# ScalarE and VectorE take over Pool's work in and around the layer norms of a decoder layer

## The chip, the cores and the metric

The kernel runs on one core of a Trainium2 chip. The metric is the device time of one execution, in microseconds; lower is better. Engines: TensorE (PE, and PEld for its weight loads), VectorE (DVE), ScalarE (ACT), GpSimd (POOL) and SyncE (SP), which issues nearly all DMAs.

## What is computed

One decoder layer on 560 tokens: 16 learned meta tokens and 512 prompt tokens, and 8 sequences of 4 new tokens with a cached window of 128. The model width is 1024, the hidden width of a feed-forward 2816, all in float32. Cut to what matters:

```python
def trunk_layer(x, ...):
    x = layer_norm(DN_ALPHA * x + 0.5 * swiglu(x, wg[0], wu[0], wd[0]), g[0], b[0])
    y, ks, vs, cs = token_mixer(x, ...)          # attention and short convolution, then w_out
    x = layer_norm(DN_ALPHA * x + y, g[1], b[1])
    x = layer_norm(DN_ALPHA * x + 0.5 * swiglu(x, wg[1], wu[1], wd[1]), g[2], b[2])

def layer_norm(x, g, b):
    mu = mean(x); var = mean((x - mu) ** 2)
    return (x - mu) * rsqrt(var + eps) * g + b
```

The change concerns the first two layer norms.

## The kernel before

**Layout.** Tokens lie along the free dimension and features along the partitions. `x_res` (128 partitions, 8 tiles of 128 features, 560 tokens) holds the residual. The tokens are worked on in two halves of 280. A "layer norm L" in the code is one norm of one half: L = 0 and 1 are the two halves of the first norm, L = 2 and 3 those of the second. For L = 2 and 3 the meta tokens are no longer needed, so L = 2 has 264 columns.

**Split products.** Each float32 product is made of three TensorE products: every operand is split in a high part (`x_hi`, `w_hi`, written by ScalarE with rounding to fp32r) and the rest (`x_lo`, `w_lo`, the original less the high part, written by VectorE), and hi*hi, hi*lo and lo*hi are summed in PSUM. A weight tile of 128x1024 goes from DMA to `w_raw`, then ScalarE writes `w_hi` and VectorE `w_lo`; `more_hi` and `more_lo` are further slots of the same ring.

**Order.** Each engine has one queue whose order is written out by hand; the engines are tied by counting semaphores. An instruction whose wait is not met holds all behind it on its engine. SP loads a weight when `w_lo` of the earlier weight in that buffer has been written (`lo_ready`).

**A layer norm L**, tile by tile (c = 0 to 7):
- `residual` (VectorE, L1901 or L1904): adds TensorE's result to `x_res`. A running sum over the tiles goes to `ln_sum`: for L = 0 and 1 VectorE makes it (L1911 copy, L1914 add), for L = 2 and 3 Pool's `residual_sum` (L2333, L2337). The last tile is not in the sum; it enters the mean as a second product.
- `ln_mean` (TensorE, L903 and L904), `ln_center` (VectorE, L1920), `ln_square` (ScalarE, L1466), `ln_sum_squares` (Pool three adds, L2352, VectorE three, L1929), `ln_var` (TensorE, L913), `ln_std` (ScalarE, L1476), `ln_rstd` (VectorE, L1933).
- `ln_scale` (VectorE, L1940): `x_res` times gain and 1/std. `ln_hi` (ScalarE, L1483): `x_hi` = `x_res` + bias. `ln_lo` (VectorE, L1947): `x_lo` = (`x_res` + bias) - `x_hi`. `ln_apply` interleaves scale c+1 with lo c. TensorE's next products wait for `x_ready`, which `ln_lo` counts.
- `residual_shift` (Pool, L2325): once `x_lo` of a tile is written, `x_res` = `x_res` + bias, for the next residual. `res_biased` counts it; the output projection's residuals and `combinations` (L1811 to L1816, sums of quadrants of `x_res` for the second feed-forward) wait for it.

**Where the four lie.** L = 0: in the last quarter of the first feed-forward's down projection (`down(0)`), in pieces of 3, 3 and 2 tiles (`LN_PIECES`), each behind a residual (with its sum) of the other half and a weight split; then TensorE starts the input projection, which waits for all eight tiles. L = 1: at the start of the input projection, all eight tiles at once; TensorE works on half 0 meanwhile. L = 2: inside the output projection. That has 16 steps k, eight output tiles for each half; for L = 2 the residual of step k is tile k, for L = 3 tile k - 8. Its norm is applied in pieces of two tiles behind steps 10 to 13 (`WO_PIECES`). L = 3: at the start of the second feed-forward. TensorE works on half 0, with `ln_mean(3)` put behind tile 3 of its first product. VectorE: `ln_center`, `ln_sum_squares`, `ln_rstd`, `hidden` (L1796, `h_f`), four tiles, `hidden`, four tiles, then the splits of hidden values (L1802), weights (L1769), block sums (L1761), combinations and `hidden` of half 1, for which TensorE's first pair step waits.

VectorE's queue in a step of the output projection:

```python
residual(2 + k // KT, k % KT, wo_bank(k), T_WO + k + 1, first=k % KT == 0, last=k % KT == KT - 1)
...
split_after(T_WO + k)                 # w_lo of the weight four ahead
if s % 2:
    attention(s // 2, odd=True)
if k in WO_PIECES:
    ln_apply(2, WO_PIECES[k])
```

ScalarE has in the same order `split_after` (`w_hi`) and `ln_hi`. Pool's queue is: the squares and the shift of L = 0, the same of L = 1, the convolutions, the residual sums of the 16 steps with the squares of L = 2 at k = 8, the squares of L = 3, the shifts of L = 2 and then L = 3, and gains and biases of the last norm.

Of the kernel before, what the change touches and what calls it, by code (L numbers as in the profile page):

```python
# [22 lines left out]
ACT = mybir.ActivationFunctionType  # L23
F32 = mybir.dt.float32
# [30 lines left out]
KT = D_MODEL // P  # L55
# [233 lines left out]
def r_count(L, c):  # L289

    return r_at("wo", L - 2 + c // KT, c % KT) if L in (2, 3) else r_at(L // 4, 1, c, L % 2)


def sum_count(L, c):

    if L >= 2:
        return (KT - 1) * L + c + 1
    return 1 + (2 * c + L if c < 2 else 2 + c + L * (KT - 3))


R_FREE = 4
# [16 lines left out]
def build(nc, x_prompt, x_sample, cache_k, cache_v, state_conv, meta_tokens, rel_bias, w_in, conv_w,  # L318
# [4 lines left out]
    with ctx:  # L323
# [7 lines left out]
        x_res = sb("x_res", [P, KT, TOK])  # L331
# [205 lines left out]
        def ln_cols(L):  # L537
            return cols(L % 2, L >= 2)

        def ln_width(L):  # L540
            return width(L % 2, L >= 2)
# [89 lines left out]

            return POOL_LO.index(n) + 1

        POOL_SUMS = (2, 3)

        def y_bank(t, b):

# [706 lines left out]
        def _(act):  # L1344
# [133 lines left out]
            def ln_hi(L, chunks):  # L1478

                for c in chunks:  # L1480
                    act.wait_ge(scaled, 8 * L + c + 1)
                    b = B0 + 8 * (L // 2) + c
                    nc.scalar.activation(x_hi[:, c, ln_cols(L)], x_res[:, c, ln_cols(L)], ACT.Identity,  # L1483
                                         bias=coef[:, b:b + 1]).then_inc(x_hi_done, 1)

            def rows_std(t):

# [244 lines left out]
        def _(dve):  # L1732
# [160 lines left out]
            def residual(L, c, bank, step, first=False, last=False):  # L1893

                half = L % 2
                dve.wait_ge(steps_done, step)
                x = x_res[:, bass.ds(c, 1), ln_cols(L)]
                a = banks[:, bank, 0:ln_width(L)].unsqueeze(1)
                s = ln_sum[:, half:half + 1, 0:ln_width(L)]
                if L in (2, 3):  # L1900
                    nc.vector.scalar_tensor_tensor(x, x, ALPHA, a, ALU.mult, ALU.add).then_inc(r_done, 1)  # L1901
                else:
                    dve.wait_ge(r_done, r_at(L // 4, 0, c, half))
                    nc.vector.tensor_tensor(x, x, a, ALU.add).then_inc(r_done, 1)  # L1904
                if last or L in POOL_SUMS or L >= 4:
                    return
                dve.wait_ge(r_done, r_count(L, c))
                if first:
                    if L >= 2:
                        dve.wait_ge(var_done, L - 1)  # L1910
                    nc.vector.tensor_copy(s, x).then_inc(sum_done, 1)  # L1911
                else:
                    dve.wait_ge(sum_done, sum_count(L, c - 1))
                    nc.vector.tensor_tensor(s, s, x, ALU.add).then_inc(sum_done, 1)  # L1914
# [27 lines left out]

            def ln_lo(L, chunks):
                for c in chunks:
                    b = B0 + 8 * (L // 2) + c
                    dve.wait_ge(x_hi_done, KT * (2 + L) + c + 1)
                    nc.vector.scalar_tensor_tensor(x_lo[:, c, ln_cols(L)], x_res[:, c, ln_cols(L)],  # L1947
                                                   coef[:, b:b + 1], x_hi[:, c, ln_cols(L)].bitcast(F32),
                                                   ALU.add, ALU.subtract).then_inc(x_ready, 1)

            def ln_apply(L, chunks):

# [363 lines left out]

        @block.gpsimd
        def _(pool):
            def residual_shift(L):

                for c in range(KT):
                    pool.wait_ge(x_ready, KT * (2 + L) + c + 1)
                    b = B0 + 8 * (L // 2) + c
                    x = x_res[:, c, ln_cols(L)]
                    nc.gpsimd.tensor_scalar(x, x, coef[:, b:b + 1], None, ALU.add).then_inc(res_biased, 1)  # L2325

            def residual_sum(L, c):

                s = ln_sum[:, L % 2, 0:ln_width(L)]
                pool.wait_ge(r_done, r_count(L, c))  # L2330
                if c == 1:
                    pool.wait_ge(var_done, L - 1)
                    nc.gpsimd.tensor_tensor(s, x_res[:, 0, ln_cols(L)], x_res[:, 1, ln_cols(L)], ALU.add  # L2333
                                            ).then_inc(sum_done, 2)
                else:
                    pool.wait_ge(sum_done, sum_count(L, c - 1))
                    nc.gpsimd.tensor_tensor(s, s, x_res[:, c, ln_cols(L)], ALU.add).then_inc(sum_done, 1)  # L2337

            def weight_lo(n):

                pool.wait_ge(hi_ready, n + 1)
                k = (KT - POOL_TILES) * P
                nc.gpsimd.tensor_tensor(split_lo(n, 1)[:, 0, k:], raw((n, ""), 1)[:, 0, k:],
                                        split_hi(n, 1)[:, 0, k:].bitcast(F32), ALU.subtract).then_inc(lo_pool, 1)

            def ln_sum_squares(L):
                s = ln_sum[:, L % 2, 0:ln_width(L)]
                for c in range(1, 4):
                    pool.wait_ge(squared, KT * L + c + 1)
                    if c >= 2:  # L2350
                        pool.wait_ge(sq_pool, 3 * L + c - 1)
                    nc.gpsimd.tensor_tensor(s, squares_of(L, 0) if c == 1 else s, squares_of(L, c), ALU.add  # L2352
                                            ).then_inc(sq_pool, 1)

            def convolve(e):
                c, half = CONV_ORDER[e]
                pool.wait_ge(z_dve, step_count("h", c, half))
                if e >= 1:
                    pool.wait_ge(taps_added, 2 * e)
                if c >= 2:  # L2360
                    pool.wait_ge(z_dve, step_count("bg", c - 2, half))
                n = HALF if half == 0 else PROMPT - HALF
                for j in range(3):
                    w = C0 + CT * j + c
                    at = half * HALF + j
                    last = nc.gpsimd.tensor_scalar(taps[:, j, 0:n], u_p[:, c, at:at + n], coef[:, w:w + 1], None, ALU.mult)
                    if half:
                        last = nc.gpsimd.tensor_scalar(
                            taps[:, j, n:HALF].rearrange("p (b t) -> p b t", b=DEC_BATCH),
                            u_s[:, c, :, j:j + DEC_SEQ], coef[:, w:w + 1], None, ALU.mult)  # L2370
                last.then_inc(taps_done, 1)
                pool.wait_ge(taps_done, e + 1)
                nc.gpsimd.tensor_tensor(taps[:, 0, :], taps[:, 0, :], taps[:, 1, :], ALU.add).then_inc(taps_added, 1)
                pool.wait_ge(taps_added, 2 * e + 1)
                nc.gpsimd.tensor_tensor(conv[:, half, c % 2, :], taps[:, 0, :], taps[:, 2, :], ALU.add
                                        ).then_inc(taps_added, 1)

            for n in range(4):
                weight_lo(n)
            pool.wait_ge(coef_ready, 1)  # L2380
            for L in range(2):
                ln_sum_squares(L)
                residual_shift(L)
            for m in range(AB, len(WI_STEPS)):
                u, half = WI_STEPS[m]
                if WI_ORDER[u][0] == "h":
                    if m == WI_STEPS.index((WI_ORDER.index(("h", 0)), 0)):
                        pool.wait_ge(zero_done, 2)
                        pool.wait_ge(kct_copied, 1)
                    convolve(CONV_ORDER.index((WI_ORDER[u][1], half)))  # L2390
            for k in range(WO_STEPS):
                if 1 <= k % KT <= KT - 2:
                    residual_sum(2 + k // KT, k % KT)
                if k == 8:
                    ln_sum_squares(2)
            ln_sum_squares(3)
            residual_shift(2)
            residual_shift(3)
            pool.wait_ge(norm_rows_in, 32)
            for half in range(2):  # L2400
                for i, (t, b) in enumerate(y_units(half, True)):

                    w, feats = Y_TILES[t][2], slice(512 * b, 512 * b + 512)
                    y = y_rows[0:w, t, feats]
                    pool.wait_ge(rows_normed, 2 * half + i + 1)
                    nc.gpsimd.tensor_tensor(y, y, g_row[0:w, feats], ALU.mult).then_inc(rows_pool, 1)
                    pool.wait_ge(rows_pool, 2 * half + i + 1)
                    nc.gpsimd.tensor_tensor(y, y, b_row[0:w, feats], ALU.add).then_inc(y_pool, 1)
# [23 lines left out]
```

## Time and profile before

| | |
|---|---|
| three runs | 1047.03, 1048.84, 1049.76 us, median 1048.84 |
| the profiled execution | 1047.22 us |
| its span, first to last instruction | 1045.4 us |
| mean granted TensorE clock | 0.979 |
| busy: PE, DVE, ACT, POOL | 994.9, 692.4, 454.2, 118.1 us |

The span is what the profile's times count in: they start with its first instruction. Start and duration of an instruction are in us in a timeline; "x2" are two instructions of one kind merged, whose duration runs from the first one's start to the last one's end. Two instructions that follow one another on an engine overlap a little, so what a queue is held for is read from one start to the next.

### The profile page before, as it was taken

Reading aid. Unit: us, or ns where it says so; the run is one execution under the profiler, and the core shown is the slowest. Engines: PE = TensorE matmul, PEld = TensorE weight load, DVE = VectorE, ACT = ScalarE, POOL = GpSimd, SP = SyncE. Lnnn points to the kernel's source line nnn. Section 1 sums busy time; section 2 is a strip of 40 time slices with the busy share of each in tenths; the row PEclk is TensorE's granted clock in tenths of the full one; section 3 lists DMA queues with packets and bytes.
Section 4 is the critical chain, followed back from the end, with each engine's and each line's share of the span. In section 5 each row is a group of like instructions: output and inputs, shape, how many; then the busy total and the mean of one; then the engine's idle time right before and its main releaser. Section 6 shows DMA issues by size and latency. Waiting matters only on the chain.

```text
span 1045.4 us, 18165 instructions
## 1 busy us (share of the span) xinstructions
PE 994.9 (95%) x7526; PEld 970.0 (93%) x7526; DVE 692.4 (66%) x980; ACT 454.2 (43%) x748; POOL 118.1 (11%) x124
## 2 busy tenths in 40 slices
PE   8979999999999998899999998799999999999994
PEld 7979999999999997899988997699999999999994
DVE  5967742577876557826676578987743588775457
ACT  4535521255545234445555454455421344553330
POOL 2000000000000003505433125300000000000004
PEclk9989999999999999899999999899999999999997
DMA  9254343133225333253121445034342222336502
GB/s 255 82 117 125 116 125 102 44 91 109 81 82 182 103 100 81 80 162 86 42 81 46 139 131 177 1 103 130 103 130 62 82 81 82 90 104 186 160 2 86
DMA packets 131594, 108.19 MB, mean 103 GB/s; under 512 B 13138, under 2 KB 129590, under 8 KB 131496
## 3 DMA queue, kind: packets, MB, share of 16 engines
q1 hardware_dynamic: 130368, 105.46, 34.1%
q10 hardware_dynamic: 1144, 1.57, 1.2%
q8 instruction: 60, 0.98, 0.4%
q14 instruction: 22, 0.18, 0.1%
HBM read 103.08 MB, written 4.95 MB: 103 GB/s over the span
## 4 chain that ended last, share of the span: by engine, by line
PE 70%; DVE 20%; issue 4%; ACT 4%; DMA 1%; DVEq 0%; SPq 0%; POOL 0%; ACTq 0%
PE banks L1042 27%; PE banks L1055 24%; PE banks L878 14%; DVE w_lo L1769 4%; DVE more_raw L1761 3%; DVE w_raw L1761 2%; DVE w_sum L1761 2%; DVE w_lo L1739 2%; PE banks L1229 1%; ACT w_hi L1365 1%; DVE x_res L1940 1%; DVE more_lo L1769 1%; DVE ln_sq L1862 1%; ACT w_hi L1351 1%; DMA w_raw<-in_ffn_w_gate 1%
## 5 line engine op out<-in xcount | busy, mean ns | idle before, releaser
L1055 PE MATMUL banks<-h_hi,w_hi 128*128 128x280 f32 (+1 forms) x480 | 139.9, 291 | 0.0
L1055 PE MATMUL banks<-h_hi,w_lo 128*128 128x280 f32 (+1 forms) x480 | 139.3, 290 | 0.0
L1055 PE MATMUL banks<-h_lo,w_hi 128*128 128x280 f32 (+1 forms) x480 | 139.3, 290 | 0.0
L878 PE MATMUL banks<-x_hi,w_hi 128*128 128x280 f32 (+1 forms) x416 | 127.8, 307 | 6.3 <-DVE x_lo L1947 4.2
L878 PE MATMUL banks<-x_lo,w_hi 128*128 128x280 f32 (+1 forms) x416 | 121.6, 292 | 0.0
L878 PE MATMUL banks<-x_hi,w_lo 128*128 128x280 f32 (+1 forms) x416 | 121.5, 292 | 0.0
L1739 DVE TENSOR_TENSOR w_lo<-w_raw,w_hi 128x1024 fp32r<-128x1024 f32 (+1 forms) x66 | 81.6, 1238 | 59.1 <-ACT w_hi L1351 58.6
L1042 PE MATMUL banks<-x_hi,w_hi 128*128 128x280 f32 (+1 forms) x400 | 116.5, 291 | 1.9 <-DVE ln_sq L1862 1.5
L1042 PE MATMUL banks<-x_hi,w_lo 128*128 128x280 f32 (+1 forms) x400 | 115.8, 290 | 0.0
L1042 PE MATMUL banks<-x_lo,w_hi 128*128 128x280 f32 (+1 forms) x400 | 115.6, 289 | 0.0
L1042 PE MATMUL banks<-t_hi,w_hi 128*128 128x280 f32 x336 | 99.4, 296 | 6.2 <-issue 5.1
L1042 PE MATMUL banks<-t_lo,w_hi 128*128 128x280 f32 x336 | 99.1, 295 | 0.0
L1042 PE MATMUL banks<-t_hi,w_lo 128*128 128x280 f32 x336 | 99.0, 295 | 0.0
L1351 ACT ACTIVATE w_hi<-w_raw 128x1024 fp32r<-128x1024 f32 x66 | 68.2, 1040 | 61.5 <-PE banks L1055 39.4
L1055 PEld LDWEIGHTS banks<-h_hi,w_hi 128*128 128x128 f32 x480 | 90.7, 189 | 0.2
L1055 PEld LDWEIGHTS banks<-h_lo,w_hi 128*128 128x128 f32 x480 | 90.6, 189 | 0.1
L1055 PEld LDWEIGHTS banks<-h_hi,w_lo 128*128 128x128 f32 x480 | 90.7, 189 | 0.0
L878 PEld LDWEIGHTS banks<-x_hi,w_hi 128*128 128x128 f32 x416 | 79.6, 191 | 11.0 <-DVE x_lo L1947 6.1
L1769 DVE TENSOR_TENSOR w_lo<-w_raw,w_hi 128x1024 fp32r<-128x1024 f32 x38 | 46.5, 1223 | 59.9 <-ACT w_hi L1365 59.9
L1042 PE MATMUL banks<-x_hi,more_hi 128*128 128x280 f32 (+1 forms) x240 | 71.6, 298 | 10.4 <-DVE h_f L1796 8.3
L878 PEld LDWEIGHTS banks<-x_lo,w_hi 128*128 128x128 f32 x416 | 79.7, 192 | 1.6 <-issue 0.5
L878 PEld LDWEIGHTS banks<-x_hi,w_lo 128*128 128x128 f32 x416 | 79.6, 191 | 0.0
(240 smaller groups left out, 2694.8 us busy)
## 6 DMA issues: line engine op xcount, KB each, us to landing
w_raw<-in_ffn_w_down SPq DMA_DIRECT2D x30, 512.0 KB, 4.0
more_raw<-in_ffn_w_down SPq DMA_DIRECT2D x28, 512.0 KB, 3.6
w_raw<-in_ffn_w_gate SPq DMA_DIRECT2D x24, 512.0 KB, 4.0
w_raw<-in_ffn_w_up SPq DMA_DIRECT2D x24, 512.0 KB, 4.9
more_raw<-in_ffn_w_gate SPq DMA_DIRECT2D x20, 512.0 KB, 3.9
more_raw<-in_ffn_w_up SPq DMA_DIRECT2D x20, 512.0 KB, 5.5
w_raw<-in_w_in SPq DMA_DIRECT2D x14, 512.0 KB, 4.7
w_raw<-in_w_out SPq DMA_DIRECT2D x32, 128.0 KB, 2.9
```

The costliest lines, as they stand in the source:

```text
L878: mm = nc.tensor.matmul(out[:, 0:n], w[:, t, :], x(k), start=(k == ends[0] and w is hi and x is rhs_hi), stop=(k == ends[1] and w is lo))
L1042: mm = nc.tensor.matmul(out[:, ab, c0:HALF], w[:, k, ab * P:(ab + 1) * P], b(t, k), start=(new and k == 0 and w is hi and t[0] is x_hi), s ...
L1055: mm = nc.tensor.matmul(out, w[:, k - k0, c * P:(c + 1) * P], h[:, k, cols(half, f)], start=(k == 0 and w is hi and h is h_hi), stop=(ku = ...
L1229: mm = nc.tensor.matmul(aux[h // 2][0:nq, (h % 2) * 256:(h % 2) * 256 + la + nq], q_t[head, h, q0:q0 + nq], k_t[head, q0 - la:q0 + nq], st ...
L1351: nc.scalar.activation(split_hi(n, 1)[:, 0, 0:k], raw((n, ""), 1)[:, 0, 0:k], ACT.Copy).then_inc(hi_ready, 1)
L1365: nc.scalar.activation(split_hi(n, 1), src, ACT.Copy).then_inc(hi_ready, 1)
L1739: nc.vector.tensor_tensor(split_lo(n, 1)[:, 0, 0:k], raw((n, ""), 1)[:, 0, 0:k], split_hi(n, 1)[:, 0, 0:k].bitcast(F32), ALU.subtract).the ...
L1761: nc.vector.tensor_tensor(out, a, b, op).then_inc(blocks_summed, 1)
L1769: nc.vector.tensor_tensor(split_lo(n, 1), src, split_hi(n, 1).bitcast(F32), ALU.subtract).then_inc(lo_ready, 1)
L1862: nc.vector.tensor_tensor(c22_sb[:, :, :], c22_sb[:, :, :], x, ALU.add).then_inc(c22_done, 1)
L1940: nc.vector.scalar_tensor_tensor(x, x, coef[:, g:g + 1], rstd[:, 0:ln_width(L)], ALU.mult, ALU.mult).then_inc(scaled, 1)
```

## The change

ScalarE writes `x_res` + bias back to `x_res` itself, right behind `x_hi`, and counts `res_biased`. `x_lo` waits for that count and is `x_res` - `x_hi`. `residual_shift` is gone. `residual_sum` is gone too: `residual` on VectorE now makes the sums of L = 2 and 3. For every L the sum starts at c = 1 with tile 0 plus tile 1, where L = 0 and 1 had a copy at c = 0; `sum_count` gives the new counts. Pool keeps the squares, the convolutions and the last norm.

```diff
@@ sum_count
-    return 1 + (2 * c + L if c < 2 else 2 + c + L * (KT - 3))
+    return 2 * (L + 1) if c < 2 else 3 + c + L * (KT - 3)
@@
-        POOL_SUMS = (2, 3)
@@ ln_hi (ScalarE)
-                    nc.scalar.activation(x_hi[:, c, ln_cols(L)], x_res[:, c, ln_cols(L)], ACT.Identity,
-                                         bias=coef[:, b:b + 1]).then_inc(x_hi_done, 1)
+                    x = x_res[:, c, ln_cols(L)]
+                    nc.scalar.activation(x_hi[:, c, ln_cols(L)], x, ACT.Identity, bias=coef[:, b:b + 1])
+                    nc.scalar.activation(x, x, ACT.Identity, bias=coef[:, b:b + 1]).then_inc(res_biased, 1)
@@ residual (VectorE)
-                if last or L in POOL_SUMS or L >= 4:
+                if last or L >= 4 or first:
                     return
                 dve.wait_ge(r_done, r_count(L, c))
-                if first:
+                if c == 1:
                     if L >= 2:
                         dve.wait_ge(var_done, L - 1)
-                    nc.vector.tensor_copy(s, x).then_inc(sum_done, 1)
+                    nc.vector.tensor_tensor(s, x_res[:, bass.ds(0, 1), ln_cols(L)], x, ALU.add).then_inc(sum_done, 2)
                 else:
@@ ln_lo (VectorE)
-                    b = B0 + 8 * (L // 2) + c
-                    dve.wait_ge(x_hi_done, KT * (2 + L) + c + 1)
-                    nc.vector.scalar_tensor_tensor(x_lo[:, c, ln_cols(L)], x_res[:, c, ln_cols(L)],
-                                                   coef[:, b:b + 1], x_hi[:, c, ln_cols(L)].bitcast(F32),
-                                                   ALU.add, ALU.subtract).then_inc(x_ready, 1)
+                    dve.wait_ge(res_biased, KT * L + c + 1)
+                    nc.vector.tensor_tensor(x_lo[:, c, ln_cols(L)], x_res[:, c, ln_cols(L)],
+                                            x_hi[:, c, ln_cols(L)].bitcast(F32), ALU.subtract).then_inc(x_ready, 1)
@@ Pool: the functions and their calls
-            def residual_shift(L):
-            def residual_sum(L, c):
-                residual_shift(L)
-                if 1 <= k % KT <= KT - 2:
-                    residual_sum(2 + k // KT, k % KT)
-            residual_shift(2)
-            residual_shift(3)
```

## Rows read from the trace of the kernel before

**Rows 1.** The page: busy time of each engine, its share of the span.
```profile
PE 994.9 (95%) x7526; PEld 970.0 (93%) x7526; DVE 692.4 (66%) x980; ACT 454.2 (43%) x748; POOL 118.1 (11%) x124
```

**Rows 2.** Waits of PE in the whole span: total, times, longest.
```profile
PE banks L1042 <- DVE h_f L1796: 8.3, 2, 6.8
...
PE banks L903 <- issue: 4.5, 1, 4.5
PE banks L878 <- DVE x_lo L1947: 4.2, 2, 3.3
```

**Rows 3.** Timeline of DVE, 404 to 425: start, duration, what, idle before.
```profile
409.45 0.93 DVE L1940 SCALAR_TENSOR_TENSOR x_res<-x_res,coef,rstd 128x280 f32<-128x280 f32 x2
...
412.52 0.44 DVE L1904 TENSOR_TENSOR x_res<-x_res,banks 128x280 f32<-128x280 f32 x1
...
414.51 1.17 DVE L1940 SCALAR_TENSOR_TENSOR x_res<-x_res,coef,rstd 128x280 f32<-128x280 f32 x2
...
417.81 0.44 DVE L1904 TENSOR_TENSOR x_res<-x_res,banks 128x280 f32<-128x280 f32 x1
418.28 0.47 DVE L1914 TENSOR_TENSOR ln_sum<-ln_sum,x_res 128x280 f32<-128x280 f32 x1
418.67 1.16 DVE L1940 SCALAR_TENSOR_TENSOR x_res<-x_res,coef,rstd 128x280 f32<-128x280 f32 x2
419.76 1.40 DVE L1947 SCALAR_TENSOR_TENSOR x_lo<-x_res,coef,x_hi 128x280 fp32r<-128x280 f32 x2
```

**Rows 4.** Timeline of ACT, 404 to 447.
```profile
411.52 0.53 ACT L1483 ACTIVATE x_hi<-x_res,coef 128x280 fp32r<-128x280 f32 x1 [0.58 <-DVE x_res L1940]
411.96 1.04 ACT L1351 ACTIVATE w_hi<-w_raw 128x1024 fp32r<-128x1024 f32 x1
...
427.79 0.75 ACT L1466 ACTIVATE silu_g<-x_res 128x280 f32<-128x280 f32 x2
```

**Rows 5.** Timeline of POOL: one of the residual sums, and the shifts.
```profile
623.48 0.79 POOL L2337 TENSOR_TENSOR ln_sum<-ln_sum,x_res 128x280 f32<-128x280 f32 x1 [2.21 <-DVE x_res L1901]
...
644.62 19.02 POOL L2325 TENSOR_SCALAR x_res<-x_res,coef 128x264 f32<-128x264 f32 x16
```

**Rows 6.** Timeline of DVE, 612 to 648.
```profile
620.54 1.42 DVE L1940 SCALAR_TENSOR_TENSOR x_res<-x_res,coef,rstd 128x264 f32<-128x264 f32 x2
...
623.50 1.85 DVE L1739 TENSOR_TENSOR w_lo<-w_raw,w_hi 128x1024 fp32r<-128x1024 f32 x1
...
636.07 1.84 DVE L1739 TENSOR_TENSOR w_lo<-w_raw,w_hi 128x1024 fp32r<-128x1024 f32 x1
637.84 0.43 DVE L1901 SCALAR_TENSOR_TENSOR x_res<-x_res,banks 128x280 f32<-128x280 f32 x1
638.19 1.21 DVE L1739 TENSOR_TENSOR w_lo<-w_raw,w_hi 128x1024 fp32r<-128x1024 f32 x1
```

**Rows 7.** The scales of line L1940, ns: minimum, median, maximum.
```profile
L1940 DVE SCALAR_TENSOR_TENSOR x_res<-x_res,coef,rstd x32: 477/505/1020, 409.5 to 657.7; 128x280 f32<-128x280 f32 x24, 128x264 f32<-128x264 f32 x8
```

**Rows 8.** Timeline of DVE, 404 to 447: first scale and last x_lo of L = 1.
```profile
435.56 0.93 DVE L1940 SCALAR_TENSOR_TENSOR x_res<-x_res,coef,rstd 128x280 f32<-128x280 f32 x2
...
443.53 0.51 DVE L1947 SCALAR_TENSOR_TENSOR x_lo<-x_res,coef,x_hi 128x280 fp32r<-128x280 f32 x1 [0.17 <-ACT x_hi L1483]
```

**Rows 9.** Timeline of ACT, 612 to 648.
```profile
621.59 0.92 ACT L1483 ACTIVATE x_hi<-x_res,coef 128x264 fp32r<-128x264 f32 x2 [3.38 <-DVE x_res L1940]
```

**Rows 10.** Timeline of DVE, 648 to 672.
```profile
650.41 1.15 DVE L1940 SCALAR_TENSOR_TENSOR x_res<-x_res,coef,rstd 128x280 f32<-128x280 f32 x2
...
665.28 1.31 DVE L1811 TENSOR_TENSOR t_raw<-x_res 128x1120 f32<-128x1120 f32 x1
```

**Rows 11.** Timeline of ACT, 648 to 672.
```profile
658.80 0.72 ACT L1386 ACTIVATE h_hi<-h_f 128x264 fp32r<-128x264 f32 x2
```

**Rows 12.** Busy time by stretch: us, engines (instructions), granted clock, DMA share, GB/s.
```profile
421.30:427.00 5.70, 5.70 (x21) 5.16 (x22) 2.33 (x7) 0.83 (x3) 1.77 (x3) 0.50 0.01 1
```

**Rows 13.** Waits of DVE, 575 to 612: total, times, longest.
```profile
DVE w_lo L1739 <- ACT w_hi L1351: 6.1, 9, 0.7
```

More of the change, by code:

```diff
@@ L2318, in _ @@
         def _(pool):
-            def residual_shift(L):
[L2321 to L2325, printed above, removed]
-            def residual_sum(L, c):
[L2329 to L2337, printed above, removed]
             def weight_lo(n):
```

## Prediction

> **What bounds the kernel now.** Start with the page [rows 1]: TensorE is busy for 95% of the span, ScalarE for 43 and Pool for 11. So time is made in the few places where TensorE stands still. The waits of PE [rows 2] name them: 6.8 us for h_f behind layer norm 3, 4.5 us for the mean of layer norm 3 ("issue"; which instruction was late is read below), 3.3 us for x_lo behind layer norm 0. All three sit in or right behind a layer norm that the change edits, and in all three it is VectorE's queue that is late. The other waits are not touched. Between the stalls TensorE is back to back, so a delay at one stall is added to the end, and delays at different stalls add up.
>
> I call layer norm L's stretch A (L=0, from 409.45), B (L=1, from 435.56), C (the second half of the output projection, with layer norm 2's pieces in it, from 615) and D (L=3, from 650.41).
>
> **The parts.** Two edits. First: Pool's 32 shifts go; ScalarE issues a second ACTIVATE for each tile behind its x_hi, and x_lo waits for that second one, and becomes a plain subtraction. Second: Pool's 12 sums go and VectorE makes them in its own queue. (The two copies that VectorE drops for layer norms 0 and 1 lie about 50 us ahead of A where VectorE is not late: nothing.) No DMA is added or moved; SP's loads are released by VectorE's w_lo, which shift with the rest and have microseconds to spare.
>
> Unit costs. A ScalarE x_hi of 280 columns lasts 0.53 us, and the next operation starts 0.44 behind its start (411.52 to 411.96) [rows 4]; the second write has the same shape and a bias pointer, so I take 0.43 from start to start, and 0.53 for who waits for it. It is not in the trace. Below it the bound is 0.37: two squares of the same width, without a bias pointer, take 0.75 together (427.79) [rows 4]. Above it is 0.53, if the two operations do not overlap at all. The value is nearest the first row, which is the same operation, so I take that. The Trainium skill's "ScalarE: Activation LUTs" (What ACT_TABLE_LOAD costs) gives 280 ns plus 0.833 ns a column with a pointer bias, and an overlap of 93 ns; its Rules for kernel authors budget the whole 0.53 an operation. The first agrees with the 0.53 and the 0.44 of the rows. By the budget the sum would be that of the second rival. On VectorE, a sum on an x_res just written starts 0.47 behind the start of that write (417.81 to 418.28) and holds the queue 0.39 more (to 418.67) [rows 3]; the write alone would have held it 0.35, so each sum costs 0.51 us of queue. This is the form of layer norm 0's own sum, so only the place is new. x_lo as a subtraction has two full operands of 280 columns as well, and I take 0.36 from start to start, as for the write.
>
> Relief from Pool. A w_lo lasts 1.85 or 1.84 when a Pool sum starts beside it and 1.21 when none does [rows 5, 6]: 0.63 each, and from start to start the 1.21 hold the queue for 1.14 (as 1.84 held it for 1.77, 636.07 to 637.84). The scale of layer norm lasts 0.48 at best and up to 1.02 [rows 7], so each that meets Pool gets back up to half a microsecond.
>
> A, pieces of 3, 3 and 2 tiles. Before: scale at 409.45, residual (L1904) at 412.52, so 3.07 [rows 3], of which 0.54 until x_hi starts (a scale of 0.51 and the handover) and 2.53 from there. After, from the first x_hi at 0: second write 0.43, x_hi 0.87, write 1.30; the first x_lo at 0.99, third scale 1.35 to 1.86, its x_hi 1.89, write 2.32 to 2.85, x_lo 2.88, residual 3.24. Plus 0.71. The second piece the same, less 0.24, because its scales (1.17 for two beside Pool, 0.93 without) start x_hi earlier. The last piece, before: 418.67 to 421.16 (419.76 + 1.40), 2.49 [rows 3]. After: x_hi at 0.53, write 0.96, x_hi 1.40, write 1.83 to 2.36, x_lo 2.39 to 2.83. Plus 0.34. A: 0.71 + 0.71 - 0.24 + 0.34 = 1.5 us, and the wait of PE grows from 3.3 to 4.8.
>
> B. Before, 8 tiles from 435.56 to the last x_lo's end 444.04 (443.53 + 0.51) [rows 8]: 8.48, or 1.06 a tile. After, ScalarE sets the pace: 16 operations of 0.43, one copy of q between (about 0.3), 0.54 ahead, waits of some 0.2 for a scale and 0.45 of x_lo behind: 8.6. Plus 0.15: here Pool's going pays for ScalarE's work.
>
> C, the largest. VectorE's order for each step is residual, w_lo of a later weight, two scales, two x_lo. The Pool sum did not gate the mean: it is late because the last residual starts at 637.84 [rows 6]. Before, a cycle is 4.19 (from 623.50 to 636.07 are three). After, from ScalarE's first x_hi of a piece: four operations, the last 1.25 to 1.76; x_lo 1.79, residual 2.15, sum 2.62, w_lo 3.01 (w_hi, 1.04 long from 1.67, is ready by then, so VectorE sets it), 1.14 of w_lo, 0.48 of scale: next x_hi at 4.61. So 0.42 more a cycle, three times: 1.26; that is two writes and a sum, less Pool's 0.63. Ahead of it two sums (k=9, 10) cost 1.02, and the scale at 620.54, 1.05 from its start to x_hi at 621.59 [rows 9], needs 0.51: 0.48 left. Behind it, from the last x_hi to the last residual, 0.49 more. C: 0.48 + 1.26 + 0.49 = 2.2 us. The other six sums (k=1 to 6) lie in the first half, where w_lo waits up to 0.7 us for w_hi behind each residual, 6.1 us in nine waits [rows 13]: nothing; without that cover 6 x 0.51 = 3.1.
>
> D. Before, the first scale at 650.41, ScalarE's h_hi at 658.80 [rows 10, 11]: 8.39. After, by the walk of A with two runs of four tiles: the x_hi start at 0.53, 1.40, 2.41, 3.28, then, behind a silu, an x_lo, an h_f and a scale, at 5.51, 6.38, 7.39 and 8.26, and two operations later (0.87) h_hi at 9.13. Plus 0.74. All that follows hangs on h_hi: w_hi, w_lo, block sums, combinations, h_f, TensorE. Pool's last shift ends at 663.64 (644.62 + 19.02) [rows 5] and the combinations that wait for it start at 665.28 [rows 10], so Pool held nobody by its result; it only slows neighbours, for which I take 0.15 off. D: 0.6.
>
> Sum: 1.5 + 0.15 + 2.2 + 0.6 = 4.4 us. The profiled execution took 1047.22 (span 1045.4, 1.8 around it), so it would take 1051.7. It is 1.6 under the median of 1048.84, so against that: 1053.
>
> The Trainium skill's "GPSIMD Engine Reference" (Specifications) says that GpSimd shares its SBUF interfaces with VectorE's instructions with two SBUF inputs. It speaks for this change; the rows of w_lo agree, and had I left the relief out, C alone would be 2.5 dearer.
>
> **Rivals.** *The second write is hidden* (not slower). Its wait gates nothing, because VectorE's queue is full meanwhile. For it: a tile took 1.06 in B, above two writes (0.87). Against it: without Pool VectorE needs only about 0.42 + 0.36 = 0.78 a tile; it decides at a ScalarE pace of 0.39 an operation, and pieces of two or three tiles have a first and a last with nothing beside them. Then relief and sums remain. A: 0.24, and 0.5 in the last piece (2.49, of which a good half a microsecond is Pool's), -0.7. B: 7 scales back by 0.2, less what TensorE can use, -0.7. C: the cycle is 4.19 - 0.63, and VectorE with the sum some 0.2 above it, so 0.45 less, four times, against the 0.48 ahead of it: -1.3. D: 0.2 a tile, half of them, -0.8. Together -3.5: 1045.3.
>
> *ScalarE's operations do not overlap.* Each then costs 0.1 more; on the path some 13 in A, 9 in B, 11 in C, 15 in D: 4.8 more, 1058. Only the budget above speaks for it, and row 411.96 against.
>
> *The clock gives some back.* After its wait of 3.3 us TensorE ran at a granted clock of 0.50, the lower level of 1.2 GHz, until 427 [rows 12]: 5.7 us at half speed, and it is on the path then. Where it returned to full speed has to do with what PE did before, and the change moves that. If the stretch behind A's shifted stall is half as long, a quarter of its length comes back: 4.4 - 1.4 = 3.0, 1051.8. In C it may as well cost 1 more. The rows don't say which way it falls.
>
> **How the numbers follow.** Forecast 0.57, with a range of its own of 1051 to 1056: at 0.37 an operation some 25 on the path are 0.06 cheaper, 1.5 less; if w_lo's 1.85 were the loads' doing and not Pool's, four times 0.63 come on top, 2.5 more. Hidden write 0.13; no overlap 0.10; clock gives back 0.20. What a measurement of this kernel can tell from no change is 0.3%, 3.1 us: the borders are 1045.7 and 1052.0. Slower: 0.52 of the forecast, 0.10, and 0.03 of the clock, 0.65. Same: 0.05, 0.05 of the hidden write and 0.17 of the clock, 0.27. Faster: the rest of the hidden write, 0.08. The range leaves out most of the hidden write (0.13) and half of no overlap (0.05): 1047.5 to 1057. Likeliest 1053.
>
> **What would show it.** Pool empty in B and C save for the squares and the taps; w_lo at 1.22 throughout C and its cycle near 4.6; PE's waits 4.8 (x_lo), 6.7 (mean) and about 7.4 (h_f) in place of 3.3, 4.5 and 6.8; ScalarE's pairs 0.43 apart. A second write that starts more than 0.45 behind x_hi, a w_lo still at 1.85, or a sum that fits in a gap of C would prove that step wrong. The whole is wrong if VectorE's queue in C gets no longer, or if TensorE's three waits grow and something behind them has the time to give back.

## The result and the profile after

The kernel became slower by a little: the median of 12 runs is 1051.74 us, against 1047.86 for the kernel before in runs beside it. The ratio is 1.0038 with a 95% interval of 1.0030 to 1.0045, or +3.9 us with bounds of 3.1 and 4.7. The prediction was +4.4 us and "slower". (One run of the twelve stood at 1104 us, and one of an experiment below at 3398; the ratios leave such runs out.) The profiled execution took 1051.29 us, 4.1 above that of before; the sum in the prediction had 1051.7. Its span is 1049.4 us and its granted clock 0.978.

The page of the changed kernel, busy times:

```profile
PE 997.2 (95%) x7526; PEld 972.6 (93%) x7526; DVE 689.6 (66%) x990; ACT 466.6 (44%) x780; POOL 70.3 (7%) x80
```

Against [rows 1], Pool lost 48 us of work, and ScalarE has 12 more. VectorE has ten more instructions and yet 3 us less busy time, since w_lo, the scales and x_lo have each become shorter (the 32 scales alone 3.1 us together). The totals say nothing about the time; the waits do. Waits of PE in the changed kernel: total, times, longest.

```profile
PE banks L1041 <- DVE h_f L1796: 8.3, 2, 6.7
PE banks L902 <- issue: 6.7, 1, 6.7
PE banks L877 <- DVE x_lo L1946: 5.5, 3, 4.1
```

The order of [rows 2] is kept, and two of the three have grown: the mean from 4.5 to 6.7 (2.2 more), x_lo from 3.3 to 4.1. The third, h_f, has not grown, although D, the stretch that leads to it, became longer, as the timelines show.

A, VectorE's timeline of the changed kernel, first and last piece:

```profile
409.71 0.93 DVE L1940 SCALAR_TENSOR_TENSOR x_res<-x_res,coef,rstd 128x280 f32<-128x280 f32 x2
411.24 0.45 DVE L1946 TENSOR_TENSOR x_lo<-x_res,x_hi 128x280 fp32r<-128x280 f32 x1 [0.59 <-ACT x_res L1484]
...
413.49 0.44 DVE L1904 TENSOR_TENSOR x_res<-x_res,banks 128x280 f32<-128x280 f32 x1
...
420.08 0.92 DVE L1940 SCALAR_TENSOR_TENSOR x_res<-x_res,coef,rstd 128x280 f32<-128x280 f32 x2
421.60 0.45 DVE L1946 TENSOR_TENSOR x_lo<-x_res,x_hi 128x280 fp32r<-128x280 f32 x1 [0.59 <-ACT x_res L1484]
422.44 0.45 DVE L1946 TENSOR_TENSOR x_lo<-x_res,x_hi 128x280 fp32r<-128x280 f32 x1 [0.39 <-ACT x_res L1484]
```

The brackets are the new wait: 0.59 us on ScalarE's write behind a pair of scales, and 0.39 before the last tile of a piece. From the first scale to the end of the last x_lo there are 13.18 us (409.71 to 422.89); before there were 11.71 (409.45 to 421.16) [rows 3]. That is 1.47 more.

C, VectorE's timeline of the changed kernel, one cycle and the end, and ScalarE's of the same piece:

```profile
621.33 1.22 DVE L1739 TENSOR_TENSOR w_lo<-w_raw,w_hi 128x1024 fp32r<-128x1024 f32 x1
622.47 0.89 DVE L1940 SCALAR_TENSOR_TENSOR x_res<-x_res,coef,rstd 128x264 f32<-128x264 f32 x2
623.95 0.43 DVE L1946 TENSOR_TENSOR x_lo<-x_res,x_hi 128x264 fp32r<-128x264 f32 x1 [0.59 <-ACT x_res L1484]
624.76 0.43 DVE L1946 TENSOR_TENSOR x_lo<-x_res,x_hi 128x264 fp32r<-128x264 f32 x1 [0.38 <-ACT x_res L1484]
625.11 0.44 DVE L1901 SCALAR_TENSOR_TENSOR x_res<-x_res,banks 128x280 f32<-128x280 f32 x1
625.59 0.45 DVE L1914 TENSOR_TENSOR ln_sum<-ln_sum,x_res 128x280 f32<-128x280 f32 x1
625.95 1.22 DVE L1739 TENSOR_TENSOR w_lo<-w_raw,w_hi 128x1024 fp32r<-128x1024 f32 x1
...
640.95 0.44 DVE L1901 SCALAR_TENSOR_TENSOR x_res<-x_res,banks 128x280 f32<-128x280 f32 x1
```

```profile
622.99 0.52 ACT L1483 ACTIVATE x_hi<-x_res,coef 128x264 fp32r<-128x264 f32 x1 [3.88 <-DVE x_res L1940]
623.41 0.50 ACT L1484 ACTIVATE x_res<-x_res,coef 128x264 f32<-128x264 f32 x1
```

From w_lo to w_lo a cycle lasts 4.62 us, where it lasted 4.19 [rows 6]. Every w_lo is at 1.22. The last residual starts at 640.95, 3.11 later than in [rows 6]; 0.90 of that C was handed at its start.

In the first half of the output projection the sums cost nothing. A sum and the w_lo behind it, timeline of VectorE:

```profile
587.85 0.43 DVE L1914 TENSOR_TENSOR ln_sum<-ln_sum,x_res 128x264 f32<-128x264 f32 x1
588.54 1.22 DVE L1739 TENSOR_TENSOR w_lo<-w_raw,w_hi 128x1024 fp32r<-128x1024 f32 x1 [0.26 <-ACT w_hi L1350]
```

The wait for w_hi that was 0.7 [rows 13] is now 0.26. The same w_lo started at 587.63 before; it is 0.9 later, which is what B had handed on, and no later by the sum.

D, VectorE's timeline:

```profile
653.88 0.92 DVE L1940 SCALAR_TENSOR_TENSOR x_res<-x_res,coef,rstd 128x280 f32<-128x280 f32 x2
...
669.21 1.32 DVE L1811 TENSOR_TENSOR t_raw<-x_res 128x1120 f32<-128x1120 f32 x1
```

15.33 us against 14.87 [rows 10]: 0.46 more.

### The profile page after: what moved, and what is told of

It reads as the page before. It is cut to its first block and busy times, and to the rows that moved or that the text cites. A ratio compares the mean times of both kernels' runs of the same rounds, so it can differ in the third digit from the quotient of the medians.

```text
span 1049.4 us, 18163 instructions
## 1 busy us (share of the span) xinstructions
PE 997.2 (95%) x7526; PEld 972.6 (93%) x7526; DVE 689.6 (66%) x990; ACT 466.6 (44%) x780; POOL 70.3 (7%) x80
## 5 line engine op out<-in xcount | busy, mean ns | idle before, releaser
L1739 DVE TENSOR_TENSOR w_lo<-w_raw,w_hi 128x1024 fp32r<-128x1024 f32 (+1 forms) x66 | 79.1, 1200 | 56.0 <-ACT w_hi L1350 55.9
```

The lines of the kernel that those rows point to most:

```text
L1739: nc.vector.tensor_tensor(split_lo(n, 1)[:, 0, 0:k], raw((n, ""), 1)[:, 0, 0:k], split_hi(n, 1)[:, 0, 0:k].bitcast(F32), ALU.subtract).the ...
```

## The experiments

**Theory:** the write that ScalarE makes in front of x_lo is a delay in VectorE's queue wherever tiles come in short pieces; the leaving of Pool gives part of it back. **Rivals:** the sums on VectorE are what costs; the write's placing doesn't matter, only that ScalarE has 32 operations more; the clock made the difference. All ratios are to the kernel before, in runs on the same chip (the experiments ran on three chips).

**Each edit alone.** The write on ScalarE, with the sums left on Pool:

```diff
@@ residual (VectorE)
-                if last or L >= 4 or first:
+                if last or L >= 2 or first:
@@ Pool's walk through the output projection
+                if 1 <= k % KT <= KT - 2:
+                    residual_sum(2 + k // KT, k % KT)
```

> The first edit alone: ScalarE writes the biased residual and x_lo waits for it, Pool still makes the output projection's sums. Theory (the write in front of x_lo is the cost, and moving the sums gives a part of it back): about +5 us over the kernel before, near 1053, so dearer than both edits together; in the output projection a cycle of 5.0 us (1.77 for w_lo beside the Pool sum, 0.51 for the scale, 1.67 for four ScalarE operations, 1.04 for w_hi) in place of 4.19 before and 4.62 after, PE's wait for the mean near 7.8. Rival (the sums on VectorE are the cost, the write is hidden): cycle 4.2, at most +1.5 us.

1053.13 us, ratio 1.0046 (1.0033 to 1.0058): the highest of all, though its interval overlaps that of the changed kernel. VectorE's timeline in C, with Pool's sum beside w_lo again:

```profile
624.28 1.80 DVE L1739 TENSOR_TENSOR w_lo<-w_raw,w_hi 128x1024 fp32r<-128x1024 f32 x1 [0.16 <-ACT w_hi L1350]
...
629.24 1.79 DVE L1739 TENSOR_TENSOR w_lo<-w_raw,w_hi 128x1024 fp32r<-128x1024 f32 x1 [0.16 <-ACT w_hi L1350]
```

The cycle is 4.96, longer than with the sums on VectorE (4.62), so the sums on VectorE are not what costs.

The sums on VectorE, with shift and x_lo as before the change:

```diff
@@ ln_hi, ln_lo as before the change; Pool
+            def residual_shift(L):
+                for c in range(KT):
+                    pool.wait_ge(x_ready, KT * (2 + L) + c + 1)
+                    b = B0 + 8 * (L // 2) + c
+                    x = x_res[:, c, ln_cols(L)]
+                    nc.gpsimd.tensor_scalar(x, x, coef[:, b:b + 1], None, ALU.add).then_inc(res_biased, 1)
```

> The second edit alone: VectorE makes the sums, Pool still shifts the residual, x_lo waits for x_hi only. Theory: w_lo falls from 1.85 to 1.22 and the cycle to about 3.9 us; two sums ahead of the pieces cost 1.0, less 0.5 for the first scale; so between -1.2 and 0 us, near 1047.2, PE's wait for the mean near 3.8. Rival (sums are the cost): cycle above 4.19 and +1.5 to +2.5 us.

1046.15 us, ratio 0.9988 (0.9980 to 0.9997): 1.3 us faster, small but outside the interval. VectorE's timeline in C:

```profile
624.28 1.22 DVE L1738 TENSOR_TENSOR w_lo<-w_raw,w_hi 128x1024 fp32r<-128x1024 f32 x1
...
626.49 0.90 DVE L1946 SCALAR_TENSOR_TENSOR x_lo<-x_res,coef,x_hi 128x264 fp32r<-128x264 f32 x2 [0.18 <-ACT x_hi L1482]
...
628.15 1.22 DVE L1738 TENSOR_TENSOR w_lo<-w_raw,w_hi 128x1024 fp32r<-128x1024 f32 x1
```

The cycle fell to 3.87. Giving VectorE a sum shortens its own queue here. Pool's sum had stretched each w_lo by 0.63, and it had also put w_lo off; in the kernel before, 0.54 us lay between the starts of the residual and of w_lo, where a residual alone holds the queue for 0.35:

```profile
622.96 0.44 DVE L1901 SCALAR_TENSOR_TENSOR x_res<-x_res,banks 128x280 f32<-128x280 f32 x1
623.50 1.85 DVE L1739 TENSOR_TENSOR w_lo<-w_raw,w_hi 128x1024 fp32r<-128x1024 f32 x1
```

With VectorE's own sum between them it is 0.84. So the sum costs 0.30 more and gives 0.63 back.

**The write behind x_lo.** Both moves, but the write is its own step on ScalarE, which waits until x_lo is done. It stands where ScalarE is early: a step after each piece, and for L = 3 behind the conversion of the next weight.

```diff
@@ ScalarE
+            def ln_shift(L, chunks):
+                for c in chunks:
+                    act.wait_ge(x_ready, KT * (2 + L) + c + 1)
+                    b = B0 + 8 * (L // 2) + c
+                    x = x_res[:, c, ln_cols(L)]
+                    nc.scalar.activation(x, x, ACT.Identity, bias=coef[:, b:b + 1]).then_inc(res_biased, 1)
@@ its calls: L = 0, 1, 2 and 3
+                    if e - 1 in LN_PIECES:
+                        ln_shift(0, LN_PIECES[e - 1])
+                if m < 4 + KT:
+                    ln_shift(1, [m - 4])
+                if k - 1 in WO_PIECES:
+                    ln_shift(2, WO_PIECES[k - 1])
+                if f:
+                    ln_shift(3, range(KT))
@@ ln_lo (VectorE): adds the bias itself, as before the change
```

> Both moves, but ScalarE's write goes behind x_lo and behind the next w_hi, into its idle time; x_lo adds the bias itself, as before. Theory: Pool's interference is gone and nothing waits for the write: A 0.5 to 0.7 us shorter than before, the second stretch 0.5, the output projection 0.7, the last one 0.8; together -2 to -3 us, 1045 to 1046. If what made the changed kernel slow were ScalarE's extra work and not its place in front of x_lo: +2 us or more.

1043.63 us, ratio 0.9960 (0.9946 to 0.9974). That beats both kernels; it is -4.2 us where -2 to -3 was expected, with an interval from -5.7 to -2.7. ScalarE has the same 32 operations more, so their number is not the cost. Waits of PE, and ScalarE's timeline at the eight writes of L = 3:

```profile
PE banks L1041 <- DVE h_f L1811: 8.1, 2, 6.5
...
PE banks L902 <- issue: 3.7, 1, 3.7
PE banks L877 <- DVE x_lo L1962: 3.3, 2, 2.6
```

```profile
657.57 3.45 ACT L1493 ACTIVATE x_res<-x_res,coef 128x280 f32<-128x280 f32 x8
```

All three waits are below those of [rows 2]. The eight writes end at 661.02, and VectorE's combinations, which read them, start at 661.30 without waiting.

**No write at all.** The same, but nobody adds the bias to the residual, and the waits for it are gone; the bias is missing from the residual stream.

> VectorE makes the sums and nobody writes the biased residual: the residual goes without the bias of layer norms 0 to 3 into the next sums, all else is computed. It is the floor for any place of the shift. Theory: within 0.5 us of the kernel with the late write, about -3 us (1045). If Pool's shifts did not disturb VectorE: as with the sums alone, about 1047.

1043.68 us, ratio 0.9960 (0.9948 to 0.9973), the same as with the late write. The traces say it more closely: A, B and D are as long in both (10.97, 7.36 and 13.84 us from the first scale), and from B to the end TensorE is never more than 0.2 us apart. So the late write is free as far as can be measured. Against the kernel with the sums alone (0.9988), what differs is Pool's 32 shifts: 0.0028, or 2.9 us, uncertain by about 1.6, which they took from VectorE beside them although nobody waited for their result. With the sums alone A, B and D last 11.71, 8.49 and 14.56 us, so the shifts made them 0.74, 1.13 and 0.72 longer, 2.6 together, and C's cycle is 3.87 with them and without. (In these two executions another 0.6 of TensorE's lead arose behind A, where the lower clock, of which more below, lasted 6.8 us with the shifts and 3.4 without. That part need not be the shifts'.)

**The early write, one layer norm at a time.** Each of these four kernels is the one with the late write, with ScalarE's write put back in front of x_lo in a single layer norm:

```diff
@@ ln_hi (ScalarE), here for L = 2
+                    if L == 2:
+                        x = x_res[:, c, ln_cols(L)]
+                        nc.scalar.activation(x, x, ACT.Identity, bias=coef[:, b:b + 1]).then_inc(res_biased, 1)
@@ ln_lo (VectorE)
+                    if L == 2:
+                        dve.wait_ge(res_biased, KT * L + c + 1)
+                        nc.vector.tensor_tensor(x_lo[:, c, ln_cols(L)], x_res[:, c, ln_cols(L)],
+                                                x_hi[:, c, ln_cols(L)].bitcast(F32), ALU.subtract).then_inc(x_ready, 1)
+                        continue
@@ the call of ln_shift for that L is gone
```

L = 2 (C):

> As the kernel with the late write, but for layer norm 2 alone (inside the output projection) the write goes back in front of x_lo, as in the changed kernel. Theory (costs of the stretches add up): the cycle there is 4.62 again instead of 3.87, four times 0.75, so +3.0 us over the late write: ratio to before 0.999, about 1046.6. If TensorE's stalls could absorb a part of it, or the cost sat in the other three layer norms: under +1.5 us.

L = 0 (A):

> The late-write kernel, with ScalarE's write back in front of x_lo for L = 0 alone. The late-write kernel goes from the first scale of A to the end of the last x_lo in 10.97 us (409.20 to 420.17), the changed kernel in 13.18 (409.71 to 422.89). Theory: this stretch returns to 13.2, TensorE's wait for x_lo grows from 2.6 to 4.8 or less, and the end comes 2.2 us later: ratio to the kernel before 0.998 (1045.4 if the late-write kernel's 0.996 holds). Both kernels had about 3.4 us of half clock behind this stall, so nothing is taken or given by the clock. Rival (the clock gives some back, and more than the kernel before suggests): under 1.6 us later, with a half-clock stretch that is shorter than 3.4 us by what is missing. Rival (A's delay is made good by a later stall): the mean of layer norm 3 or h_f waits less by the same amount and the ratio stays 0.996.

L = 1 (B):

> The late-write kernel, with the write in front of x_lo for L = 1 alone. First scale to end of the last x_lo: 7.36 us late-write, 8.55 changed. Theory (every such delay reaches the end): +1.2 us, ratio 0.997. Rival (B has slack, because what follows it waits for something else first): no change, 0.996, although the stretch is 1.2 us longer.

L = 3 (D):

> The late-write kernel, with the write in front of x_lo for L = 3 alone. First scale to first combination: 13.84 us late-write (647.46 to 661.30), 15.33 changed (653.88 to 669.21). Theory: +1.5 us, ratio 0.9975, with TensorE's longest wait for h_f between 6.5 and 8.0. Rival (D has slack in front of h_f): no change, 0.996. With the piece for L = 2 measured before (+3.7) the four should add up to the 8.2 us between the late-write kernel and the changed one: 2.2 + 1.2 + 3.7 + 1.5 = 8.6.

Measured. "Stretch" is VectorE's own, between marks of its timeline: first scale to end of last x_lo (A, and B to the mark right behind it), reciprocal to last residual (C), h_f ahead of the first scale to first combination (D). The last column is the ratio less 0.9960, times 1047.

| early write in | stretch, late write | stretch | difference | ratio (interval) | by the ratio |
|---|---|---|---|---|---|
| A | 10.97 | 13.18 | 2.21 | 0.9991 (0.9981–1.0001) | 3.2 |
| B | 7.32 | 8.51 | 1.19 | 0.9969 (0.9958–0.9981) | 0.9 |
| C | 20.42 | 23.42 | 3.00 | 0.9995 (0.9986–1.0003) | 3.7 |
| D | 14.18 | 15.69 | 1.51 | 0.9979 (0.9970–0.9989) | 2.0 |

The stretches came out as expected. Whether each reached the end the ratios show only in part: with the uncertainty of both ratios every number of the last column is uncertain by some 1.7 us, and B's 0.9 can't be told from nothing. TensorE's own timeline is closer. Its products ran later than with the late write by 1.2 us in front of A and 3.4 behind it, by 0.4 and 1.1 around B, by 0.8 and 3.8 around C, and by 1.2 and 2.7 around D: 2.2, 0.7, 3.0 and 1.5 reached it. Its wait for the mean went from 3.7 to 6.7 with the early write in C. VectorE's timeline for A, beginning and end:

```profile
410.36 0.93 DVE L1956 SCALAR_TENSOR_TENSOR x_res<-x_res,coef,rstd 128x280 f32<-128x280 f32 x2
...
422.25 0.45 DVE L1963 TENSOR_TENSOR x_lo<-x_res,x_hi 128x280 fp32r<-128x280 f32 x1 [0.59 <-ACT x_res L1488]
423.09 0.45 DVE L1963 TENSOR_TENSOR x_lo<-x_res,x_hi 128x280 fp32r<-128x280 f32 x1 [0.39 <-ACT x_res L1488]
```

The rival that a later stall makes A's delay good falls: the mean still waits 3.7 and h_f 6.5. Only B has part of it made good on the way. Between the mark behind B (L = 1) and the reciprocal in C lie 172.53 us, where the kernel with the late write has 173.00; so some 0.5 of 1.19 is made good, which fits the 0.9 of its ratio.

The four ratios add up to 9.8 us, the stretches to 7.9 (7.4 with B's 0.5 off), and the step from the late write to the changed kernel is 8.2 (1.0038 less 0.9960). Each ratio is uncertain by about 1 us and all share that of the late write, so the two sums can't be told apart. Of A the ratio gave 1.0 more than its stretch, which is within the uncertainty. The profiled execution had also lost 1.16 us before the reciprocal ahead of A (405.75 against 404.59), on which the edit has no hold: TensorE had waited 3.2 us for the loads of the input at the start, against 0.9 with the late write, and was 1.0 us behind at 62 us already.

**A piece moved out of the mean's way.** The late write again, and L = 2's last piece and the last w_lo go behind the last residual and behind the centring:

```diff
-        WO_PIECES = {10: range(0, 2), 11: range(2, 4), 12: range(4, 6), 13: range(6, 8)}
+        WO_PIECES = {10: range(0, 2), 11: range(2, 4), 12: range(4, 6), 15: range(6, 8)}
@@ Vector's order around the centring of layer norm 3
+                    weight_lo(U_GU[1] + 3)
@@ VectorE, step k of the output projection
-                split_after(T_WO + k)
+                if k < WO_STEPS - 1:
+                    split_after(T_WO + k)
@@ ScalarE, ahead of its eight writes of L = 3
+                    ln_shift(2, range(6, KT))
```

> The late write, and in the output projection the last two tiles of layer norm 2 (tiles 6, 7) go behind the last residual instead of ahead of it, with VectorE's last w_lo behind the centring of layer norm 3. Theory (VectorE's queue ahead of the last residual is what the mean waits for): the last residual comes some 2 us earlier, PE's wait for the mean falls from 3.7 to about 1.7; the centring starts 0.8 to 1.5 us earlier and the end follows: 0.8 to 1.5 us faster than the late write, ratio to before near 0.995. If the mean waited for something else, or if what follows waits for w_lo: no gain.

1042.0 us, ratio 0.9957 (0.9942 to 0.9972): not to be told from the late write alone. Waits of PE, and its product for the variance of layer norm 3:

```profile
PE banks L1041 <- DVE h_f L1812: 8.7, 2, 7.1
...
PE banks L912 <- issue: 2.5, 2, 1.8
...
PE banks L902 <- issue: 1.8, 1, 1.8
```

```profile
643.09 0.71 PE L912 MATMUL banks<-ln_sum,mean_of 128*128 128x280 f32 x2 [1.81 <-issue]
```

The mean's wait fell from 3.7 to 1.8 as meant, but a new wait of 1.8 for the variance stands behind it, and h_f is waited for 0.6 longer. The moved w_lo makes the first: it holds VectorE's queue from 639.16 to 640.86, between the centring and VectorE's share of the sum of squares, for which the variance waits. The centring began 1.36 us earlier than with the late write (636.31 against 637.67), the reciprocal only 0.34 (644.84 against 645.18). The second comes of VectorE, which now does wait at the combinations for ScalarE, since that has ten writes to make there:

```profile
661.53 1.32 DVE L1827 TENSOR_TENSOR t_raw<-x_res 128x1120 f32<-128x1120 f32 x1 [0.49 <-ACT x_res L1494]
```

Most of the gain was given back at once, by the same queue. Something may be left: this execution came to the output projection 1.1 us behind that of the late write and to the combinations 0.23 behind (661.53 against 661.30), so it made good some 0.8 us, the lower end of what was expected and less than the ratios can show. It is also the only one of the executions in which the clock did not fall behind the stall of C.

## Why the prediction was right, and where it was off

**The mechanism** was the one forecast: with the write in front, ScalarE's pace sets VectorE's queue at the edges of each piece, and Pool's leaving pays for only a part. In three one-edit steps from the kernel before, by the ratios: sums to VectorE −1.3, Pool's shifts away −2.9, ScalarE's writes in front of x_lo +8.2; together +4.0 (the second and third are uncertain by some 1.5 us each). The middle term is a real relief that the writes' placing overpaid.

**The unit costs.** ScalarE's two operations lie 0.42 apart in C (622.99 to 623.41), and 0.42 to 0.44 in A and D, where a tile has 280 columns, against 0.43 forecast. The no-overlap rival falls with that: it asked for 0.53. The write that the rows of before did not have lasts 0.50 to 0.52. The sum holds the queue from 625.11 to 625.95 with its residual, 0.84, where 0.35 + 0.51 was forecast. w_lo fell by 0.63. The Trainium skill's "ScalarE: Activation LUTs" (What ACT_TABLE_LOAD costs) gives 93 ns of overlap between activations, and the changed kernel agrees (0.52 long, the next one 0.42 after its start).

**The terms.** A 1.47 (1.52 forecast), B 0.07 (0.15), C 2.21 (2.23), D 0.46 (0.60). Together 4.2 against 4.5 (the prediction's 4.4 rounds the terms). In C the cycle was forecast at 4.61 and is 4.62. The gloss on it, "two writes and a sum, less Pool's 0.63", does not add up to the 0.42 of the walk, though: 0.86 + 0.51 - 0.63 is 0.74. From start to start, x_lo comes 0.41 later behind x_hi, and the residual 0.34 later behind x_lo, which is what the two writes cost; w_lo comes only 0.30 later behind the residual, for Pool's sum had held it back already, and 0.63 comes off. D's difference is the relief, for which I took 0.15: h_hi came 0.69 later by the walk (0.74 forecast), and the block sums and w_lo behind it gave back 0.23, as two of them took 2.36 instead of 2.58.

**What was off.** The step "the waits grow by as much as the stretch": forecast were 4.8 for x_lo and about 7.4 for h_f, and they are 4.1 and 6.7. The stretches did grow, but a wait is the difference of two times, and TensorE's own last work also ended later. In A the last x_lo was ready 1.73 later (422.89 against 421.16), and TensorE stopped 0.9 later (4.1 and 3.3 before those times), which leaves 0.8. It ended later because it waits for the same queue: a product of the down projection needs the bank that the residual behind A's first piece reads, and ran at 413.99 instead of 413.04, after a wait of 0.52 for x_res that the kernel before did not have. In D the 0.46 was waited for ahead of the long wait, at tiles of x_lo: 0.21 and 1.19 us (at 656.00 and 660.87), where there had been one wait of 0.91. The mean's 6.7 came out as forecast. The waits alone would have understated A and missed D; the marks on VectorE's timeline did not.

**The clock.** Behind the stall of A the granted clock was at 0.50 (1.2 GHz) from 423.7 to 427.1, where before it was so for twice as long, 6.8 us (most of it in [rows 12]), and of the 1.73 by which x_lo was late only 1.10 was left at the centring of layer norm 1, and 0.92 at the first scale of B (436.48 against 435.56). The rival had 1.4 come back; it was 0.8. Behind the stall of C it went the other way: the lower level until 645.6, and 0.43 us lost by the centring of layer norm 3. Windows of the changed kernel: the second column is the length, PEclk the third number from the end.

```profile
423.70:427.10 3.40, 3.40 (x13) 2.88 (x12) 1.11 (x4) 0.63 (x2) 0.00 (x0) 0.50 0.00 0
...
638.70:645.60 6.90, 4.12 (x14) 3.63 (x15) 5.66 (x12) 2.57 (x4) 0.52 (x1) 0.51 0.56 165
...
672.89:683.13 10.24, 5.67 (x24) 5.70 (x25) 10.21 (x12) 6.13 (x10) 0.00 (x0) 0.50 0.00 0
```

The last of them lies behind the stall of D, where the kernel before had 6.8 us of it (669.5 to 676.4). It cost nothing: TensorE's products ran 5.2 us later than before up to 685.9, but 4.0 at 686.1, since the kernel before waits 1.0 us there for w_lo and the changed one does not. So the rival's mechanism was there, in both directions, and half of the gift was taken back. That it belongs to the change is not borne out. The kernels with the late write, and with the early write in B alone, have the same code in C. Windows of the one and of the other, behind the same stall:

```profile
634.90:638.30 3.40, 2.87 (x8) 2.39 (x9) 2.19 (x5) 0.42 (x2) 0.00 (x0) 0.50 0.74 225
```

```profile
635.30:642.10 6.80, 5.57 (x21) 5.08 (x22) 5.21 (x11) 2.87 (x8) 1.37 (x2) 0.50 0.74 225
```

In the second the clock stayed low for 6.8 us instead of 3.4, and from the centring (637.67 and 638.77) to the reciprocal (645.18 and 647.31) there are 7.51 and 8.54 us: 1.0 lost to the clock by one execution and not by the other. The stretch behind A differed in the same way between kernels with the same code there. The chance of 0.20 that I gave the clock was for a gift that the measured time would show; what the executions show is a spread of about half a microsecond to one for each stall, in either direction. How much of the measured 3.9 us is the clock's is open. The mean granted clock of the changed kernel's runs has a median of 0.975, that of the 53 runs of the kernel before in the experiments 0.979, which leaves room for a part. What decides in an execution was not tested.

**The hidden write** was the other side's rival. It needed ScalarE to be ahead of VectorE at the edges of the pieces, and the brackets of 0.59 and 0.39 show that it was behind. The kernel with the late write shows what the rival promised: −3.5 worked out, −4.2 measured (−5.7 to −2.7).

## What to carry to other kernels

An operation whose result nobody needs soon should not stand between two that somebody waits for, even on an engine that is 44% busy: the same 32 writes cost 8.2 us in front of x_lo and nothing that could be measured behind it. Taking work off Pool can be worth more than its results suggest (2.9 us here for shifts that nobody waited for), so price a neighbour by what it does to the instructions beside it, and try the parts of a two-part change apart. To see a small delay, measure between marks on the queue that sets the stall, since the wait itself also moves with whoever waits.

## What the runs showed of the hardware

- A VectorE subtraction of 128x1024 takes 1.22 us alone and 1.79 to 1.85 beside a Pool addition of 128x280 that takes 0.79 [rows 5, 6]. Over a cycle it was cheaper for VectorE to make the addition itself (3.87 us against 4.19).
- The granted clock behind a stall stayed at its lower level for 3.4 us in one execution and 6.8 in another where the code was the same, and that moved what followed by up to 1.0 us. It is likely a part of why the 53 executions of the kernel before in the experiments lie between 1044.35 and 1049.27 us: the three with a mean granted clock of 0.984 took 1045.60 or less, the twelve with 0.977 took 1047.41 or more. No experiment isolates it.
